# One decoder layer on one core: an earlier load of the last combination, and PSUM banks of their own for two steps of the attention heads

## What is computed

```python
h = _rms_norm(x, p['g_mix'], RMS_EPS)
z = h @ p['w_in']                                  # [pool | q1,q2 | k1,k2 | v | two gates]
q = _rope(z[..., OFF_Q:OFF_K].reshape(B, T, N_HEADS, 2, HEAD_DIM), pos)
k = _rope(z[..., OFF_K:OFF_V].reshape(B, T, N_HEADS, 2, HEAD_DIM), pos)
v = z[..., OFF_V:OFF_G].reshape(B, T, N_HEADS, 2 * HEAD_DIM)
# per head: p = softmax(mask(q k^T / 8)) for both maps; a = p1 - lam * p2; o = a v
o = _rms_norm(o, p['g_subln'], SUBLN_EPS) * (1.0 - lam_init)
merged = gate_pool * (pool_out @ p['w_pool_proj']) + gate_attn * (o @ p['w_attn_proj'])
x = x + merged @ p['w_o']
h2 = _rms_norm(x, p['g_mlp'], RMS_EPS)
x = x + jnp.square(jax.nn.relu(h2 @ p['w_up'])) @ p['w_down']
```

## Time and profile before

| | |
|---|---|
| median of 3 runs | 1711.43 us (1710.4 to 1711.77) |
| the profiled execution | 1712.73 us, of which its span is 1710.7 us |
| busy, share of the span | PE 1667.7 us (97%), DVE 1188.4 (69%), ACT 736.9 (43%), POOL 133.7 (8%) |
| chain that ended last | PE 89%, DVE 6%, issue 2%, ACT 2%, DMA 1% |
| mean granted clock of TensorE | 0.993 |

### The profile page before, as it was taken

How to read it: one execution, slowest core, us unless ns; L and a number is a source line. 1 busy time by engine, 2 the same in 40 slices (tenths; PEclk the granted TensorE clock), 3 DMA queues, 4 the chain that set the end, 5 groups by cost and what they waited for, 6 DMA issues and landing times.

```text
span 1710.7 us, 30509 instructions
## 1 busy us (share of the span) xinstructions
PE 1667.7 (97%) x12112; PEld 1614.6 (94%) x12112; DVE 1188.4 (69%) x1978; ACT 736.9 (43%) x1512; POOL 133.7 (8%) x244
## 2 busy tenths in 40 slices
PE   7999999999989999999999999999999999999988
PEld 7889889889878999999999999999999999999987
DVE  6677777777776788765444458777676786868686
ACT  4455555555554321265311345334433553544343
POOL 3212212222210000000000000000000000000001
PEclk9999999999999999999999999999999999999999
DMA  6202202201213527665412222444444733444223
GB/s 205 63 2 75 63 16 72 75 23 54 69 32 104 182 93 229 204 216 173 142 50 62 75 87 66 158 148 154 138 136 137 280 123 119 155 157 137 92 75 125
DMA packets 153212, 195.22 MB, mean 114 GB/s; under 512 B 7785, under 2 KB 121385, under 8 KB 151016
## 3 DMA queue, kind: packets, MB, share of 16 engines
q1 hardware_dynamic: 138352, 160.56, 29.4%
q10 hardware_dynamic: 14720, 32.72, 5.3%
HBM read 149.35 MB, written 44.13 MB: 113 GB/s over the span
## 4 chain that ended last, share of the span: by engine, by line
PE 89%; DVE 6%; issue 2%; ACT 2%; DMA 1%; POOL 0%; DVEq 0%; ACTq 0%; POOLq 0%
PE ps L1171 34%; PE ps L931 23%; PE ps L836 16%; PE ps L862 3%; PE ps L895 3%; PE ps L885 2%; PE ps L1224 1%; PE ps L1281 1%; PE ps L1078 1%; DVE kv_pages L1962 1%; DVE w_lo L1780 1%; PE ps L866 1%; DVE mx L1837 1%; PE ps L806 0%; DMA d_raw<-ff_plain_scratch 0%
## 5 line engine op out<-in xcount | busy, mean ns | idle before, releaser
L836 PE MATMUL ps<-w_hi,h_hi 128*128 128x384 f32 x520 | 182.3, 351 | 4.7 <-DVE w_lo L1780 2.7
L836 PE MATMUL ps<-w_hi,h_lo 128*128 128x384 f32 x520 | 176.8, 340 | 0.0
L836 PE MATMUL ps<-w_lo,h_hi 128*128 128x384 f32 x520 | 176.0, 338 | 0.0
L1171 PE MATMUL ps<-d_hi,m_hi 128*128 128x258 f32 x784 | 158.8, 284 | 5.3 <-DVE m_lo L2189 2.6
L1171 PE MATMUL ps<-d_lo,m_hi 128*128 128x258 f32 x784 | 159.2, 285 | 0.0
L1171 PE MATMUL ps<-d_hi,m_lo 128*128 128x258 f32 x784 | 158.2, 283 | 0.0
L1361 ACT ACTIVATE prob<-ps,nbias 128x256 f32<-128x256 f32 (+7 forms) x128 | 94.9, 742 | 84.8 <-DVE nbias L1840 82.4
L1171 PEld LDWEIGHTS ps<-d_hi,m_hi 128*128 128x128 f32 x784 | 121.6, 190 | 6.0 <-DVE x L2356 3.0
L1171 PEld LDWEIGHTS ps<-d_hi,m_lo 128*128 128x128 f32 x784 | 122.4, 190 | 0.0
L1171 PEld LDWEIGHTS ps<-d_lo,m_hi 128*128 128x128 f32 x784 | 121.8, 190 | 0.0
L1578 ACT ACTIVATE m_hi<-m_pair 128x512 fp32r<-128x512 f32 (+1 forms) x128 | 76.9, 600 | 104.3 <-PE ps L1171 91.5
(11 more groups left out here) (295 smaller groups left out, 4335.7 us busy)
## 6 DMA issues: line engine op xcount, KB each, us to landing
ff_combination_scratch<-ff_st SPq DMA_DIRECT2D x14, 1806.0 KB, 6.9
d_raw<-ff_combination_scratch ACTq DMA_DIRECT2D x21, 1032.0 KB, 7.9
w_raw<-in_w_in SPq DMA_DIRECT2D x41, 512.0 KB, 5.3
kv_pages<-in_cache_k SPq DMA_DIRECT2D x32, 512.0 KB, 5.3
kv_pages<-in_cache_v SPq DMA_DIRECT2D x32, 512.0 KB, 4.5
m_pair<-in_w_up SPq DMA_DIRECT2D x16, 1024.0 KB, 9.6
m_pair<-in_w_down SPq DMA_DIRECT2D x24, 512.0 KB, 5.4
out<-kv_st SPq DMA_DIRECT2D x16, 512.0 KB
```

Source lines behind the costliest of these rows:

```text
L836: mm = pe.matmul(bank[0:n, 0:3 * P], a[:, kt, toks(t)], w[:, :, kt, :], start=(kt == 0 and m == 0), stop=(kt == KT - 1 and m == 2))
L1171: mm = pe.matmul(acc[:, c], w[:, kt], a[:, kt % kts, c * CW:(c + 1) * CW], start=(opens and kt == 0 and m == 0), stop=(kt == n - 1 and m = ...
```

## The change

Three things are changed.

1. The samples' projection goes to bank 5 (was 3), and the seventh turn to bank 3 (was 6). The waits follow: the seventh turn no longer waits for the split of the turned weights in bank 6 but for the rotation of block 1; the scores of block 4 (block 2 in the last head) wait for the split of the seventh turn; block 1's projection waits for that split too.
2. The samples' copy on ScalarE and their rotation on VectorE move from step 8 to step 0 of the next head, behind that step's exponentials and behind its weights. Block 0 of the next projection no longer waits for them (`z_before`: -1). Block 1 does: its count, 9 * hp, includes the samples of the head before.
3. `PLAIN` is loaded at block 1 of the last span (was 6), and its pieces are split at blocks 19 and 25 (were 9 and 11).

```diff
+PLAIN_LOAD_AT, PLAIN_SPLIT_AT = 1, (19, 25)
...
-            return ps[:, 3] if t in (1, NTT) else bank_z
+            return ps[:, 3] if t == 1 else ps[:, 5] if t == NTT else bank_z
...
-            before = {0: 0, 1: 0, 2: 1, NTT: 2}.get(t, t)
+            before = {0: -1 if hp > 1 else 0, 1: 0, 2: 1, NTT: 2}.get(t, t)
             return 9 * hp + before
+
+        def turn_bank(t):
+            return ps[:, 3] if t == NTT - 1 else bank_t[1]
...
+            if c == PLAIN:
+                load_at[c], split_at[c] = before + PLAIN_LOAD_AT, [before + k for k in PLAIN_SPLIT_AT]
...
                     if hp and t == NTT:
                         pe.wait_ge(s_exp, 16 * hp)
+                    if hp and t == 1:
+                        pe.wait_ge(s_qklo, 8 * hp)
...
-                pe.wait_ge(s_qklo, 8 * h + i + 1)
+                pe.wait_ge(s_qklo, 8 * h + (NTT if i == (2 if h == HEADS - 1 else 4) else i + 1))
...
                     if t == 0:
                         need(pe, s_atlo, 12 * h)
+                    elif t == NTT - 1:
+                        pe.wait_ge(s_zfree, z_before(h + 1, 2) + 1)
...
-                    qk_transposes(h + 1, 1 - par, t)
+                    qk_transposes(h + 1, 1 - par, t, turn_bank(t))
...
+                    if s == 0 and normed:
+                        sample_low(h)
...
-                    if proj and s == NTT:
-                        sample_low(h + 1)
...
-                    if not proj and s == 0:
-                        rotate(h, par, NTT, k_par)
...
-                    if proj and (s < NTT or h + 1 < HEADS - 1):
+                    if s == 0 and normed:
+                        rotate(h, par, NTT, k_par)
+                    if proj and s < NTT:
                         rotate(h + 1, 1 - par, s, k_par)
```

More of the change, by code:

```diff
@@ L1418, in head @@
                     if proj and s >= 1:
-                        qk_high(h + 1, 1 - par, s - 1)
-                    if proj and s == NTT:
-                        sample_low(h + 1)
+                        qk_high(h + 1, 1 - par, s - 1, turn_bank(s - 1))
                     if proj and s < NTT:
@@ L1902, in head @@
                         split_qkv(h + 2, (0, 1))
-                    if proj and (s < NTT or h + 1 < HEADS - 1):
+                    if s == 0 and normed:
+                        rotate(h, par, NTT, k_par)
+                    if proj and s < NTT:
                         rotate(h + 1, 1 - par, s, k_par)
                     if proj and s >= 1:
-                        qk_low(h + 1, 1 - par, s - 1)
+                        qk_low(h + 1, 1 - par, s - 1, turn_bank(s - 1))
             def lambda_steps():
```

## The result

The changed kernel takes **1719.28 us** (median of 6 runs, 1718.35 to 1721.91) against 1711.35 us (6 runs, 1709.94 to 1712.97) of the kernel before: ratio **1.0050, 95% interval 1.0037 to 1.0063**. It is slower by about 8 us. The forecast was 1714.9, +3.4, with a range that ended at 1717.5: the direction is as foretold, the size is not. The profiled execution took 1721.91 us (span 1719.9).

The account below looks back on a forecast made before the run. TensorE, busy for 97% of the span, was taken as the bound, so only its waits could be won. Head changes +6.1, last head +0.8 and plain combination -3.5 gave +3.4 us: 1714.9, range 1707 to 1717.5.

Parts of the forecast that it names:

- The turn and block 0's projection: Each head change: the turn starts 0.34 us earlier and block 0's projection gains 0.52 more, 0.86 together.
- Block 1's projection: Each head change: it waits for the samples' copy and is released at 257.52 instead of 257.50, spending the 0.86 us gain.
- GpSimd's pair: Each head change: VectorE stands 0.96 us before block 0's rotation for GpSimd's two additions, priced at 0.85 us, bounds to 2.71.
- The first value matmul: Each head change: `aT_lo` comes 1.42 us later against 0.47 of slack, so TensorE loses 0.99 us there.
- Behind it the maxima wait for TensorE's scores again, and the lag is absorbed: After the first value matmul of each head change: no further loss from VectorE's lateness.
- Six times: Changes into heads 1 to 6: each costs 1.01 us instead of gaining 0.86, +6.1 us in all.
- The last head: Change into the last head, once: +0.8 us, between 0.3 and 1.4, the samples' rotation now standing behind the weights.
- The plain combination: Last span: -4.12 us from the old pair, +0.65 for a new wait in the last pair, net -3.5, between -4.1 and -2.5.
- the delay stops before the values: Rival, 18%: `aT_lo` comes within its slack of 0.47 us, a head change costs 0.0; 1708.9 us.
- the head changes keep their gain: Rival, 10%: the samples' copy is done before block 1 asks, saving 6 x 0.86 us; 1702.4 us.
- The third: Rival, 10%: the plain pieces stall their new pairs as much as the old one, the end gains nothing; 1718.3 us.
- The clock: Rival, 12%: longer TensorE waits lengthen the half-clock stretch early in the last head, at most 1.7 us; 1716.6 to 1718.

Follow-up runs that it names:

- e5: Changed kernel with ScalarE's samples' copy moved ahead of block 0's exponentials; 1715.25 us, ratio 1.0029 to the kernel before, head 63.85 us.
- e6: Changed kernel with own buffers for the samples' two products, so block 0's rotation needn't wait for GpSimd's additions; 1711.91 us, ratio 1.0007 to the kernel before.
- e4: Changed kernel with the samples' copy ahead of block 0's exponentials and their rotation ahead of the last head's output sum; 1703.56 us, ratio 0.9958 to before.
- e8: e4 with the multiplication by the last head's norm moved behind the weights of step 1; 1700.33 us, ratio 0.9933 to the kernel before.
- e1: Kernel before with only the plain combination's load at block 1 and pieces at 19 and 25; 1708.88 us, ratio 0.9981 to the kernel before.
- e7: Kernel before with only the seventh turn moved to bank 5; 1711.59 us, ratio 1.0003 to the kernel before.
- e3: Changed kernel, but block 1's projection no longer waits for the samples' copy; 1722.91 us, ratio 1.0071 to the kernel before.

## Why the prediction was wrong

- **The turn and block 0's projection:** right, 0.91 of gain for 0.86.
- **Block 1's projection:** the mechanism was right (it waits for the samples' copy and spends the gain), the size was not: -0.33 - 0.58 + 1.20 = **+0.29 where +0.02 was forecast**. The term that was mis-sized is `sample_low` "ahead of the copy that VectorE's sum waits for, 0.39 (250.19 to 250.58)". Before, `o_low` began 0.09 after the start of the exponential's accumulator read; now the copy begins 0.22 after that start and `o_low` 0.50 after the copy, a delay of 0.63 and not 0.39. Most of the miss is in how I read the old row: 0.39 is only the distance from the copy to the next start. There too the copy began 0.40 behind the instruction ahead of it (249.79 to 250.19), where without it the next begins 0.26 behind (254.50 to 254.76 in the new trace), so that it cost 0.53 in its old place. The other 0.10 goes with the new neighbours, and no run shows which of them does it. e5 measures 0.65 for the whole.
- **GpSimd's pair:** right, 0.45 and 0.45 us, VectorE idle for 1.04 (0.96 forecast). The reason that I gave was not exact: at 252.48 VectorE was still at `qk_lo`, and the split began at 252.66, but the addition did end 0.3 us behind it (254.78 and 254.47). The Trainium skill, "SBUF — State Buffer", section "Who interferes with whom", says that a VectorE instruction with two SBUF inputs contends with a GpSimd instruction that reads SBUF. The trace agrees: 2.30 us beside the split, 0.45 with VectorE idle. e6 shows what VectorE's wait for the pair is worth: 1.13 us a head.
- **The first value matmul:** right, 1.06 for 0.99.
- **"Behind it the maxima wait for TensorE's scores again, and the lag is absorbed":** this step failed. The maxima of block 2 start without idle time in both traces (264.50 before, 270.98 after), so they wait for no scores. Behind them VectorE stands 1.00 us for ScalarE's `o_low` in both, so VectorE, ScalarE and VectorE again form a chain in which little of the lag is made up. `rotate` of block 2 begins 6.48 us later in the new trace (268.48 before, 274.96 after) where the first value matmul ahead of it is 6.06 later, so 0.4 of lag is left, and block 3's projection had 0.1 to spare. Cost: **0.39 a head change** (0.29 late and 0.10 for starting again). e4 and e8 show the mechanism: the same loss of 0.3 stays when every other wait is gone, and goes when VectorE's idle 1.76 and the multiplication behind it leave the chain ahead of block 0's `aT_lo`.
- **Six times:** 0.27 + 0.07 + 0.39 = 0.73 too little, 4.4 us in all. That is the whole miss (7.8 by the trace, 3.4 forecast).
- **The last head:** +0.7 for +0.8. **The plain combination:** -3.4 for -3.5, and e1 -3.3; the last pair's extra 0.62 us was forecast at 0.65. In e7's trace the old waits there are 0.9 us shorter than in that of before, so the gain lies between 2.5 and 3.4 by the execution.
- **The rivals:** "the delay stops before the values" and "the head changes keep their gain" fell in the first trace. The third, that the plain pieces stall their new pairs, has the time nearest to the measured one, 1718.3, by coincidence: those pairs take 10.09 and 10.71 us, and e1 gains. The clock has no visible part in the slowdown: executions of both kernels with the same mean clock (0.992, 0.993, 0.994) differ by 8.2 to 8.8 us. It has one in e3. The range was built around the size of the middle term, whose ends I had set by 0.2 us for each head change; three errors of one sign, repeated six times, went past it, and past 1717.5 too.

## What to carry to other kernels

Waits that stand in a list one behind the other can be one delay: take one away and see whether the next grows (e3, e7), and follow the queue of the engine that releases them, not the waiting one. When work is moved into a step, put it where both its own engine and the one behind it already stand idle; here the same change cost 1.75 us a head with the samples' work in one place and gained 0.68 with it a few instructions further ahead on both engines. A price that is paid once per loop must be read as what the instruction adds between its neighbours, and from a row with the same neighbours, since its error is multiplied too; and a lag may be called absorbed only once the chain of the late engine is followed to the next place that needs it.

## What was not expected of the hardware

- A projection's first matmul can cost 0.1 us more than the wait ahead of it: 275.96 to 276.24 is 0.28 us where the same pair stood 0.18 apart (269.61 to 269.79). But where the mask's matmuls stand ahead, the first pair is 0.26 apart without a wait and 0.28 with one, so that a wait costs only 0.02 more.
- Waits of the same length (1.85 us, six times in e3) brought the half clock behind two of them and not behind the other four. By the Trainium skill, "TensorE: Matmul & The Clock Gate", section "What's actually happening", an idle array loses its full clock; the trace agrees, but a single wait of this size does it only sometimes, here two times in six, for 1.04 and 1.07 us.
- A ScalarE copy of 8 x 384 out of PSUM added 0.53 us to the queue behind a turn's copy and 0.63 behind an exponential with its accumulator read; the copy's own 0.48 us is the same in both.
